# Six of eight linear recurrences moved into the input projection of a hybrid mixer block

## The reference, cut to what matters

```python
def even_mixer(...):
    hy, rx, gate = split(h @ w_in)          # 1024 -> 3*512, 512, 512
    xc = dwconv(rx, rc_w, rc_b, 2, 1)       # 4 taps
    for d, reverse in enumerate((False, True)):
        r = sigmoid(blockdiag(xc, a_w[d]) + a_b[d])
        i = sigmoid(blockdiag(xc, x_w[d]) + x_b[d])
        a = exp(-8 * r * softplus(-lam[d]))
        b = sqrt(-expm1(2 * log(a))) * (i * xc)
        h[d] = linear_scan(a, b, h0, reverse)   # context first, its end starts the latent
    y_rg = (h[0] + h[1]) * gelu(gate)
    # Hyena: 3-tap conv of hy, split to x0, x1, v
    y_hy = x0 * bidir_fftconv(v * x1, ...)
    return concatenate([y_hy, y_rg]) @ w_out
```

## Time and profile before

| | us |
|---|---|
| median of 3 runs | 3098.6 (3098.09 to 3099.22) |
| the profiled execution | 3097.99 |
| its span on the core | 3096.1 |
| input projection, units 2 to 9 | 736.2 to 869.4 |
| turn, recurrences, forward transform | 869.4 to 981.5 |
| inverse transform | 981.5 to 1018.9 |

### The profile page before, as it was taken

The page is one execution under the profiler, slowest core; times in us unless marked ns, Lnnn a source line. Parts: engine busy times, 40 slices in busy tenths (PEclk is TensorE's granted clock), DMA queues, the critical chain, the costliest instruction groups (busy, mean ns, idle before and its releaser), DMA issues.

```text
span 3096.1 us, 43430 instructions
## 1 busy us (share of the span) xinstructions
PE 2906.1 (94%) x15883; PEld 2479.4 (80%) x15883; DVE 2034.2 (66%) x3222; ACT 1030.8 (33%) x1589; POOL 283.8 (9%) x393
## 2 busy tenths in 40 slices
PE   5999999999976999999999999999997998899997
PEld 2588999988843778999997899999865997688885
DVE  4476767775457377767677787777755887554544
ACT  0422323334144152323223333233344665322221
POOL 1000000010010101010001000000103552000000
PEclk8899999999988999999999999999997999999998
DMA  8344432221121224354421122222211000233330
GB/s 292 103 134 152 136 122 62 75 69 44 51 73 50 61 79 159 118 168 127 164 94 56 41 62 75 68 61 75 64 41 44 24 24 15 68 109 102 98 98 29
DMA packets 301111, 269.50 MB, mean 87 GB/s; under 512 B 31111, under 2 KB 257263, under 8 KB 300880
## 3 DMA queue, kind: packets, MB, share of 16 engines
q1 hardware_dynamic: 278384, 188.95, 20.5%
q0 software_dynamic: 21760, 76.03, 6.9%
q10 hardware_dynamic: 864, 3.15, 0.3%
HBM read 262.85 MB, written 5.24 MB: 87 GB/s over the span
## 4 chain that ended last, share of the span: by engine, by line
PE 86%; DVE 7%; ACT 3%; DMA 2%; issue 1%; POOL 1%; SPq 0%; ACTq 0%; DVEq 0%; POOLq 0%
PE PSALL L2687 14%; PE PSALL L2688 14%; PE PSALL L2689 14%; PE PSALL L2930 7%; PE PSALL L2931 7%; PE PSALL L2932 7%; PE PSALL L2736 2%; PE PSALL L2608 2%; PE PSALL L2737 2%; PE PSALL L2738 2%; PE PSALL L2711 2%; PE PSALL L3293 1%; PE PSALL L3278 1%; PE PSALL L2650 1%; PE PSALL L3174 1%
## 5 line engine op out<-in xcount | busy, mean ns | idle before, releaser
L1865 DVE SCALAR_TENSOR_TENSOR X<-PSALL,GATE,X 128x512 f32<-128x512 f32 x480 | 279.8, 612 | 102.5 <-PE PSALL L2689 101.7
L2930 PE MATMUL PSALL<-HHI,WSH 128*128 128x384 f32 x816 | 275.0, 337 | 5.6 <-DVE HLO L2063 5.6
L2931 PE MATMUL PSALL<-HLO,WSH 128*128 128x384 f32 x816 | 274.3, 336 | 0.0
L2932 PE MATMUL PSALL<-HHI,WSL 128*128 128x384 f32 x816 | 274.2, 336 | 0.0
L2687 PE MATMUL PSALL<-GHIA,WHIW 128*128 128x512 f32 (+1 forms) x616 | 217.8, 354 | 13.5 <-DVE X L1865 10.5
L2688 PE MATMUL PSALL<-GLOA,WHIW 128*128 128x512 f32 (+1 forms) x616 | 213.9, 347 | 0.0
L2689 PE MATMUL PSALL<-GHIA,WLOW 128*128 128x512 f32 (+1 forms) x616 | 213.3, 346 | 0.0
L2688 PE MATMUL PSALL<-GLOB,WHIW 128*128 128x512 f32 (+1 forms) x616 | 213.2, 346 | 0.0
L2689 PE MATMUL PSALL<-GHIB,WLOW 128*128 128x512 f32 (+1 forms) x616 | 213.2, 346 | 0.0
L2687 PE MATMUL PSALL<-GHIB,WHIW 128*128 128x512 f32 (+1 forms) x616 | 213.1, 346 | 0.0
L2930 PE MATMUL PSALL<-TH,WSH 128*128 128x384 f32 x612 | 208.6, 341 | 0.0
(11 more groups left out here) (380 smaller groups left out, 6963.9 us busy)
## 6 DMA issues: line engine op xcount, KB each, us to landing
RAW<-in_ffn_w_in_dram SPq DMA_DIRECT2D x176, 512.0 KB, 4.3
ADA<-in_ada_w_dram POOLq DMA_DIRECT2D x144, 512.0 KB, 5.7
RAW<-in_ffn_w_out_dram SPq DMA_DIRECT2D x88, 512.0 KB, 3.9
RAW<-in_ev_w_in_dram SPq DMA_DIRECT2D x20, 512.0 KB, 4.0
WRAW<-in_mla_w_q_up_dram SPq DMA_DIRECT2D x16, 288.0 KB, 3.0
RAW<-in_ev_w_out_dram SPq DMA_DIRECT2D x8, 512.0 KB, 5.2
RAW<-in_mla_w_in_dram SPq DMA_DIRECT2D x8, 512.0 KB, 4.4
RAW<-in_mla_w_out_dram SPq DMA_DIRECT2D x8, 512.0 KB, 4.8
```

Source lines behind the costliest of these rows:

```text
L1865: dve.scalar_tensor_tensor(X[:, m, lo:lo + n], down_bank(m, s, 2), GATE[:, j, m, s:s + 1], X[:, m, lo:lo + n], ALU.mult, ALU.add).then_inc ...
L2930: te.matmul(out, w_hi, hi[block](k), start=(k == 0), stop=False)
L2931: te.matmul(out, w_hi, low[block](k), start=False, stop=False)
L2932: x = te.matmul(out, w_lo, hi[block](k), start=False, stop=(k == 3))
```

## The change

Six of the eight recurrences (n = 0 to 5) are taken in the projection; 6 and 7 stay behind it.

- PE: the loop over units is written out. In units 4 to 9 `gates(u-4, s)` follows the first column block of each token segment. These gates go to banks 6 and 7; the second segment's wait for the sigmoids of the first.
- ACT: after its weights and its evictions of unit u, `root(u-4)` and `decays(u-3)`.
- DVE: after the convolutions of unit u, `recur(u-4)` and `decay(u-3)`. The convolutions of unit 9 and the high and low parts of the recurrences' output (`rg_parts`) come after the sixth spectrum.
- Behind the projection: DVE `recur(5)`, then for n = 6, 7 `decay(n), spectrum(n-6), recur(n)`, then spectra 2 to 5; PE `gates(6), forward(0), gates(7), forward(1)` and the other four forwards.
- Scans write over their input; the states have no tiles of their own, three `IG` take turns and `RR` is one tile. The sum of two directions is gated into `GATED`.
- `BD` lies where nothing else is at the time, and POOL zeroes and loads it once the layer norm before the projection has ended.

```diff
@@ -258,23 +258,23 @@
     XC = place("XC", [P, HC, GT_])
     GATED = place("GATED", [P, HC, GT_])
     T_ = [place(f"RT{n}", [P, GT_]) for n in range(3)]
+    BD = [place("BD0", [P, 2, P])]
     place = region(r2, TOP)
     U = place("U", [P, HC, GT_])
     X0 = place("X0", [P, HC, GT_])
     T_ += [place(f"RT{n}", [P, GT_]) for n in range(3, 9)]
-    RR, IG, AA, TH = T_[0:2], T_[2:4], T_[4:6], T_[6:8]
-    HS = [T_[8], sb("RT9", [P, GT_], F32, at=r1 + 2 * 3104)]
+    RR, IG, AA, TH, VT_ = T_[0], T_[1:4], T_[4:6], T_[6:8], T_[8]
+    BD.append(place("BD1", [P, 2, P]))
     place = region(w_at, r1)
     UT = place("UT", [P, TB, HY])
     YL = place("YL", [P, 2, LB, HY])
-    YC = [place("YC0", [P, CB_, HY]), sb("YC1", [P, CB_, HY], F32, at=r1)]
-    SLAB, KFS, TMP, BD = [], [], [], []
+    YC = [place("YC0", [P, CB_, HY]), sb("YC1", [P, CB_, HY], F32, at=r2 + 2 * 12320 + 3104)]
+    SLAB, KFS, TMP = [], [], []
     for n in range(2):
         place = region(h_at + 24576 * n, h_at + 24576 * n + 12288)
         SLAB.append(place(f"SLAB{n}", [P, 1024]))
         KFS.append(place(f"KFS{n}", [P, 2, HY]))
         TMP.append(place(f"TMP{n}", [P, HY]))
-        BD.append(place(f"BD{n}", [P, 2, P]))
...
@@ -440,6 +440,16 @@
     MLA_COLS = [QL, QL + P, QL + KVL] + [P * n for n in range(QC_)]
     NF = LB + CB_
+    RG_EARLY = 6
+    RY0 = 1 + 3 + HC
+    def gate_bank(n, s, v):
+        if n < RG_EARLY:
+            return PS[6 + v][:, 0:LAT] if s == 0 else PS[6][:, CTX * v:CTX * v + CTX]
+        return PS[v][:, 0:LAT] if s == 0 else PS[2][:, CTX * v:CTX * v + CTX]
@@ -772,8 +782,7 @@
         for n in range(3):
             pool.memset(PAD[n][:, :], 0.0).then_inc(pad_zero, 1)
-        pool.wait_ge(pe["A"], plan["ev_out"].A)
-        pool.wait_ge(pe["B"], plan["ev_out"].B)
+        pool.wait_ge(h_lo, plan["ln0"].h + 2 * KC)
         for n in range(2):
             pool.memset(BD[n][:, :, :], 0.0).then_inc(bd_zero, 1)
         pool.wait_ge(bd_zero, 2)
@@ -1232,6 +1241,37 @@
                 for half in range(2):
                     split_hi(slot, half, b.q + 2 * u + half, 0, (b.A if slot == "A" else b.B) + per * (u // 2))
...
+            def decays(n):
+                c, d = n // 2, n % 2
+                col = HC * d + c
+                early = n < RG_EARLY
+                if n == 0:
+                    act.wait_ge(r_y, 4)
+                    act.wait_ge(spl, SPL_N)
+                else:
+                    act.wait_ge(r_m, n)
+                if n >= 3:
+                    act.wait_ge(r_y, RY0 + 2 * ((n - 3) // 2 + 1))
+                for s in range(2):
+                    lo, w = GSEGS[s]
+                    act.wait_ge(gate_pe, 2 * n + s + 1)
+                    for v, (dst, bias) in enumerate(((RR, ab), (IG[n % 3], xb))):
+                        act.activation(dst[:, lo:lo + w], gate_bank(n, s, v), ACT.Sigmoid,
+                                       bias=VECS[:, bias + col:bias + col + 1]).then_inc(r_sig, 1)
+                act.wait_ge(r_sig, 4 * (n + 1))
+                if n >= 2:
+                    act.wait_ge(r_scan, 2 * (n - 1))
+                act.activation(AA[n % 2][:, :], RR[:, :], ACT.Exp, scale=SPL[:, 6, col:col + 1]).then_inc(r_exp, 1)
+                act.activation(TH[n % 2][:, :], RR[:, :], ACT.Tanh, scale=SPL[:, 7, col:col + 1]).then_inc(r_tanh, 1)
+            def root(n):
+                act.wait_ge(r_m, n + 1)
+                act.activation(TH[n % 2][:, :], TH[n % 2][:, :], ACT.Sqrt).then_inc(r_sqrt, 1)
...
+                if u >= HC - 1:
+                    if u >= HC:
+                        root(u - HC)
+                    if u < HC - 1 + RG_EARLY:
+                        decays(u - HC + 1)
             for t in range(TB):
                 act.wait_ge(ut_pe, t + 1)
                 act.activation(UT[:, t, :], PS[4 + t % 4][:, :], ACT.Copy).then_inc(ut_ok, 1)
...
-            for n in range(2 * HC):
-                c, d = n // 2, n % 2
...
-                if n >= 1:
-                    root(n - 1)
-            root(2 * HC - 1)
+            for n in range(RG_EARLY, 2 * HC):
+                decays(n)
+                root(n)
@@ -2251,45 +2271,38 @@
...
+            def unit_conv(k):
+                kind, c = CONVS[k]
+                if kind == "rg":
+                    convolve(k, XC[:, c, :])
+                elif c < HC:
+                    convolve(k, X0[:, c, :])
+                elif c < 2 * HC:
+                    convolve(k, U[:, c - HC, :])
+                else:
+                    convolve(k, VT_[:, :])
+                    step(dve.tensor_tensor(U[:, c - 2 * HC, :], U[:, c - 2 * HC, :], VT_[:, :], ALU.mult))
+                assert nc_[0] == CONV_END[k]
+                return k + 1
...
-                for half in range(1 if u < HC else 2):
-                    dve.wait_ge(mx_taken, 4 * u + 3 + half)
-                    kind, c = CONVS[k]
-                    if kind == "rg":
-                        convolve(k, XC[:, c, :])
-                    elif c < HC:
-                        convolve(k, X0[:, c, :])
-                    elif c < 2 * HC:
-                        convolve(k, AA[0][:, :])
-                    else:
-                        convolve(k, AA[1][:, :])
-                        step(dve.tensor_tensor(U[:, c - 2 * HC, :], AA[0][:, :], AA[1][:, :], ALU.mult))
...
             def decay(n):
                 c = n // 2
                 dve.wait_ge(r_sig, 4 * (n + 1))
-                dve.tensor_tensor(IG[n % 2][:, :], IG[n % 2][:, :], XC[:, c, :], ALU.mult).then_inc(r_in, 1)
+                dve.tensor_tensor(IG[n % 3][:, :], IG[n % 3][:, :], XC[:, c, :], ALU.mult).then_inc(r_in, 1)
                 dve.wait_ge(r_exp, n + 1)
                 dve.wait_ge(r_tanh, n + 1)
-                dve.tensor_tensor(RR[n % 2][:, :], AA[n % 2][:, :], AA[n % 2][:, :], ALU.mult).then_inc(r_sq, 1)
+                dve.tensor_tensor(RR[:, :], AA[n % 2][:, :], AA[n % 2][:, :], ALU.mult).then_inc(r_sq, 1)
                 dve.wait_ge(r_sq, n + 1)
-                dve.scalar_tensor_tensor(TH[n % 2][:, :], RR[n % 2][:, :], 1.0, TH[n % 2][:, :], ALU.add,
+                dve.scalar_tensor_tensor(TH[n % 2][:, :], RR[:, :], 1.0, TH[n % 2][:, :], ALU.add,
                                          ALU.mult).then_inc(r_m, 1)
@@ -2304,26 +2317,41 @@
                 c, d = n // 2, n % 2
                 dve.wait_ge(r_sqrt, n + 1)
                 dve.wait_ge(r_in, n + 1)
-                dve.tensor_tensor(IG[n % 2][:, :], IG[n % 2][:, :], TH[n % 2][:, :], ALU.mult).then_inc(r_b, 1)
+                a, h = AA[n % 2], IG[n % 3]
+                dve.tensor_tensor(h[:, :], h[:, :], TH[n % 2][:, :], ALU.mult).then_inc(r_b, 1)
                 dve.wait_ge(r_b, n + 1)
...
-                a, b, h = AA[n % 2], IG[n % 2], HS[d]
-                dve.tensor_tensor_scan(h[:, ctx], a[:, ctx], b[:, ctx], 0.0, ALU.mult, ALU.add).then_inc(r_scan, 1)
+                dve.tensor_tensor_scan(h[:, ctx], a[:, ctx], h[:, ctx], 0.0, ALU.mult, ALU.add).then_inc(r_scan, 1)
                 dve.wait_ge(r_scan, 2 * n + 1)
-                dve.tensor_tensor_scan(h[:, lat], a[:, lat], b[:, lat], h[:, end:end + 1], ALU.mult, ALU.add).then_inc(r_scan, 1)
+                dve.tensor_tensor_scan(h[:, lat], a[:, lat], h[:, lat], h[:, end:end + 1], ALU.mult, ALU.add).then_inc(r_scan, 1)
                 dve.wait_ge(r_scan, 2 * n + 2)
                 if d == 0:
                     return
-                ystep(dve.tensor_tensor(HS[0][:, :], HS[0][:, :], HS[1][:, :], ALU.add))
-                ystep(dve.tensor_tensor(HS[0][:, :], HS[0][:, :], GATED[:, c, :], ALU.mult))
+                ystep(dve.tensor_tensor(h[:, :], h[:, :], IG[(n - 1) % 3][:, :], ALU.add))
+                dve.wait_ge(mx_taken, 4 * c + 3)
+                ystep(dve.tensor_tensor(GATED[:, c, :], GATED[:, c, :], h[:, :], ALU.mult))
+            def rg_parts(c):
                 for (lo, w), (g0, _) in zip(SEGS, GSEGS):
-                    ystep(dve.tensor_copy(HHI[:, HC + c, lo:lo + w], HS[0][:, g0:g0 + w]))
-                    dve.tensor_tensor(HLO[:, HC + c, lo:lo + w], HS[0][:, g0:g0 + w],
+                    ystep(dve.tensor_copy(HHI[:, HC + c, lo:lo + w], GATED[:, c, g0:g0 + w]))
+                    dve.tensor_tensor(HLO[:, HC + c, lo:lo + w], GATED[:, c, g0:g0 + w],
                                       HHI[:, HC + c, lo:lo + w].bitcast(F32), ALU.subtract).then_inc(y_rg, 1)
-                dve.wait_ge(y_rg, 2 * c + 2)
+            k = 0
+            for u in range(9):
+                if u + 2 < 10:
+                    ev_split("ev_in", u + 2)
+                for half in range(1 if u < HC else 2):
+                    dve.wait_ge(mx_taken, 4 * u + 3 + half)
+                    k = unit_conv(k)
+                if u >= HC - 1:
+                    if u >= HC:
+                        recur(u - HC)
+                    if u < HC - 1 + RG_EARLY:
+                        decay(u - HC + 1)
...
-            for n in range(2 * HC):
```

(99 more changed lines are left out.)

## The result

The changed kernel takes 3055.6 us in the median (3053.57 to 3060.81, 4 runs) against 3098.86 us (3098.09 to 3099.22, 4 runs) for the kernel before: ratio 0.9864, 95% interval 0.9852 to 0.9876. 3059.7 was predicted, in 3052 to 3070. The profiled execution took 3056.28 us, its span is 3054.4 us.

The account below looks back on a forecast made before the run. PE bounds the projection; behind it 112.1 us are a chain of hand-overs. Before 112.1, after 15.5 + 57.7 = 73.2, gain 38.9 us: profiled 3059.1, median 3059.7 us, range 3052 to 3070.

Parts of the forecast that it names:

- Part 1, gates: Projection, PE: six gates at 2.59 us each are paid in full, 15.5 us, as PE is full there.
- Part 2, ACT and DVE: Projection: ACT's 12.1 and DVE's 16.8 us fit in a 19.25 us unit; sigmoid slack 6 us, PE never stopped.
- Part 3, the stage behind: From the projection's end to the inverse: 57.7 us instead of 112.1, with spectrum, slab, forward as what is late next.
- the list: Part 3's step-by-step end times behind the projection, counted from its end; the inverse begins at 55.7 us.
- cold starts: Behind the projection: PE gaps of 1 to 4 us cost between 0 and 6.4 us; 2 us taken.
- chain of hand-overs: Behind the projection: no engine is full in the 112.1 us, so the stage is a chain of hand-overs.
- 1 (dearer gates): Projection: gates cost more between products, 10 us more in all, 3070 us; chance 0.10.
- 2 (dearer switches): ACT: each table switch costs its 1.28 us twice, spectra 8.5 us late, 3068 us; chance 0.04.
- 3: Behind the projection: the ring of slab transfers was the bound, nothing is gained, 3095 to 3104 us; chance 0.04.
- 4: Projection: ACT's order makes PE wait for first-segment sigmoids in six units; slower, 3108 us at 8 us a unit; chance 0.04.

Follow-up runs that it names:

- doubled kernel: Every gate matmul of the six early recurrences issued twice, against the changed kernel (also called doubled gates): 3070.52 us, 16.3 more.
- order alone: Changed kernel with UT copies first, forward(0) and (1) ahead of gates(7), scans of 6 and 7 under the inverse, slab requests unchanged: 3057.19 us.
- second repeat: The changed kernel measured again with nothing altered, the second time: 3053.89 us, ratio 0.9857 to the kernel before.
- early gate weights alone: Kernel before, with only the gate weights put in places of their own and loaded ahead of the projection: 3092.55 us against 3099.44.

## Why the prediction was right

- **Part 1, gates.** 15.5 us forecast, 15.8 in the trace (115.7 - 99.95), 15.3 for six more in the doubled kernel. That nothing hides them was right, and that they have no price beyond their row.
- **Part 2, ACT and DVE.** Weights 1.1 us late: measured 1.1. Slack of the first sigmoids 6 us: measured 5.5. PE waited for nothing in the projection. One detail was off: the sigmoids' table load was thought to run while ACT waits for gates; it comes behind that wait.
- **Part 3, the stage behind.** Without the allowance for cold starts the sum was 55.7 us, and the trace has 55.7. That this fits to the tenth is luck, as errors cancel in it. gates(6) was taken as cold (done at 10.7); it was warm and done at 9.6, though its start was at 7.0, not 6.6, behind cold transposes. And the late table load put tanh(6) at 15.4 instead of 14.6, so decay(6) ended at 17.4, not 16.5. spectrum(0) was to wait for forward(0) until 17.5; it followed decay(6) instead, at 17.3. From there on the links on the chain are within 0.6 us of the list; gates(7) and forward(2), which are not on it, ended 1.1 us earlier.
- **The term that was mis-sized** is the cold starts: 2 us were added for gaps of 1 to 4 us, and no forward product was cold in this trace (with doubled gates and with the order alone forward(5) was, at 1.7 us). Without it the forecast would have been 3057.7. What was cold are the transposes, at a cost of 0.7 us that the list didn't have. The gain was put down to the chain of hand-overs; the clock has a part in it that the prediction didn't name. In the kernel before, forward(3) and forward(5) were cold too, besides the first gates and forward(2). More of the chain that ended last before the change:

```profile
891.18 1.99 ACT RT L1287 x4
...
924.53 9.33 PE PSALL L3149 x16
...
956.31 5.37 PE PSALL L3149 x8
```

  Against warm ones (2.75, 7.03, 3.67) the four took 1.5 + 1.6 + 2.3 + 1.7 = 7.1 us longer; in the changed kernel none does. forward(2) is not on the chain, which goes from gates(1) to the sigmoids and on through the recurrences, so 5.5 of the 7.1 us lay on it. They go with the shorter waits, not beside them; what the clock alone would have brought no run shows.
- **The rivals.** 1 (dearer gates) is excluded by the doubled gates; 2 (dearer switches) by the rows of ACT, where 0.01 to 0.02 us lie between a load and the activation behind it. The Trainium skill (ScalarE: Activation LUTs, What ACT_TABLE_LOAD costs) gives each switch a load of about 1283 ns and a drain of about 1380 ns; the load agrees with 1.28 us, the drain shows in no trace here. 3 was right in that the ring is the next bound, wrong in its length; its price was too low as well, as with 112 us left as they were the gates in the projection would still have cost 15.5 us, 3114 us in all. 4's mechanism is real and was produced by 9.3 us of extra work on ACT; the changed kernel is 5.5 us away from it.
- **What the prediction didn't see:** that four recurrences would have done. The prediction took the number of six as given and made no sum for fewer; the one for four, 5.2 us off the projection and 5.5 us on what follows, was made only after the result, and came out.

## What to carry to other kernels

Moving a latency chain under a stage that one engine bounds cost that engine's share of the chain here, 15.8 us for 15.5 us of gates; the idle time of the others was free as long as each hand-over had more slack than the lag it got, so work out that slack per hand-over and not from busy shares. Stop moving when the chain that stays behind fits beside its neighbour: past that point, between four recurrences and six here, each piece cost as much as it saved. Then look at what releases the next bound: here a transfer waited for the consumer of a product when it could have waited for the product itself.

## What the runs showed of the hardware that was not expected

- Plain fp32 products cost the same between fp32r products as between their own kind: 2.55 to 2.63 us for a group of eight (15.3 and 15.8 us for six groups) against 2.58 to 2.59 between forward products, with no idle time on either side.
- Waits of the same length left TensorE warm in one run and cold in another. In the changed kernel forward(5) follows 2.02 us of waiting and takes 3.70 us; with doubled gates it follows 2.05 us and takes 5.40:

```profile
946.02 5.40 PE L3186 MATMUL PSALL<-UT,SLAB 128*128 128x512 f32 x8 [2.05 <-DMA SLAB<-in_fwd_c_dram]
```

  Which wait is longer does not decide it either: forward(5) of the changed kernel was warm after 2.31 us (its second repeat), and forward(4) cold, 5.40 us, after 1.96 (early gate weights alone). The sum of such waits can so be forecast only with a margin of 1.7 us for each. The transposes show the same, 2.7 or 4.1 us from first to last behind 2.65 us of waiting.
